# First layer's projections and attention in one block, by half slabs, with five slab slots

## The reference

```python
mod = jnp.dot(jax.nn.silu(c), w_ada[l]) + b_ada[l]          # 6 x 1024 modulation values
h = rmsnorm(x, g_pre_mix[l]) * (1.0 + sc1) + sh1
z = jnp.dot(h, w_in[l])                                      # q_m k_m v_m o_m i_m f_m q_a kc vc ks vs kw vw g_a
qk = jax.nn.silu(causal_depthwise_conv(concat(q_m, k_m), conv_qk[l]))
y_m = mlstm(q_m, k_m, v_m, i_m + b, f_m + b) * jax.nn.sigmoid(o_m)          # 4 heads of 128
kc, vc = compress(kc_a, ...), compress(vc_a, ...)            # 15 compressed keys and values
y_a = nsa(q_a, kc, vc, ks, vs, kw, vw, sigmoid(g_a), rel_bias)              # 8 heads of 64, three branches
y = jnp.dot(concat(y_m, y_a), w_out[l])
x = x + gt1 * rmsnorm(y, g_post_mix[l])
h2 = rmsnorm(x, g_pre_ffn[l]) * (1.0 + sc2) + sh2
x = x + gt2 * rmsnorm(moe(h2, ...), g_post_ffn[l])           # 32 experts, top 4
# second_block: its own modulation from ada_w_2, projections, sparse attention, state-space branch
```

## Time and profile before

| what | us |
|---|---|
| runs of the kernel before, median (lowest to highest) | 1987.55 (1986.05 to 1988.58) |
| the profiled execution, its own time | 1990.91 |
| its span | 1988.9 |
| PE busy / DVE / ACT / POOL | 1822.5 / 456.5 / 319.3 / 74.4 |
| mean granted clock of PE, as a share of full speed | 0.95 |

### The profile page before, as it was taken

The page is one execution under the profiler, slowest core; times in us unless marked ns, Lnnn a source line. Parts: engine busy times, 40 slices in busy tenths (PEclk is TensorE's granted clock), DMA queues, the critical chain, the costliest instruction groups (busy, mean ns, idle before and its releaser), DMA issues. The chain is left out here.

```text
span 1988.9 us, 37739 instructions
## 1 busy us (share of the span) xinstructions
PE 1822.5 (92%) x16443; PEld 1012.4 (51%) x16443; DVE 456.5 (23%) x718; ACT 319.3 (16%) x628; POOL 74.4 (4%) x57
## 2 busy tenths in 40 slices
PE   7996576799999999999999999999949898899998
PEld 5685345433434343434344443434425787667886
DVE  1223504511101010111111111111231550443301
ACT  1102412400000000000000000000020265222200
POOL 0000000000000000000000000000000034100000
PEclk9997787799999999999999999999969899899999
DMA  8964741689999999999999999999644233132410
GB/s 283 245 234 133 269 164 36 279 341 393 397 403 391 398 401 397 402 399 399 394 404 395 405 394 404 399 397 413 260 161 165 89 127 127 43 127 103 151 43 22
DMA packets 159951, 546.34 MB, mean 275 GB/s; under 512 B 24682, under 2 KB 35194, under 8 KB 127002
## 3 DMA queue, kind: packets, MB, share of 16 engines
q1 hardware_dynamic: 136960, 524.32, 68.8%
q10 hardware_dynamic: 21786, 17.09, 2.9%
q0 software_dynamic: 1152, 4.19, 0.6%
HBM read 527.09 MB, written 17.84 MB: 274 GB/s over the span
## 5 line engine op out<-in xcount | busy, mean ns | idle before, releaser
L1319 PE MATMUL ps<-ring_low,xg 128*32 128x512 f32 x3072 | 346.8, 600 | 0.0
L1319 PE MATMUL ps<-second_ring,xg 128*32 128x512 f32 x3072 | 335.4, 592 | 0.0
L1319 PEld LDWEIGHTS ps<-second_ring,xg 128*32 128x32 f32 x3072 | 99.5, 110 | 230.1 <-issue 230.1
L1319 PEld LDWEIGHTS ps<-ring_low,xg 128*32 128x32 f32 x3072 | 97.0, 111 | 208.7 <-issue 203.0
L1450 DVE TENSOR_SCALAR gl<-ps 128x768 f32<-128x768 f32 x32 | 30.6, 958 | 686.9 <-PE ps L1319 686.9
L1342 PE MATMUL ps<-second_ring,aT 128*32 128x256 f32 x3072 | 173.3, 382 | 2.3 <-ACT aT L1401 2.3
L1342 PE MATMUL ps<-raw_more,aT 128*32 128x256 f32 x3072 | 171.6, 379 | 0.0
L1342 PEld LDWEIGHTS ps<-second_ring,aT 128*32 128x32 f32 x3072 | 100.4, 111 | 82.5 <-issue 20.2
L1342 PEld LDWEIGHTS ps<-raw_more,aT 128*32 128x32 f32 x3072 | 99.9, 110 | 65.9
L1395 ACT ACTIVATE sg<-gl 128x768 f32<-128x768 f32 x32 | 27.0, 845 | 512.2 <-DVE gl L1450 512.2
L277 PE MATMUL ps<-hT,second_ring 128*128 128x256 f32 x448 | 98.2, 380 | 1.5 <-PEq L1549 1.5
(11 more groups left out here) (469 smaller groups left out, 1665.0 us busy)
## 6 DMA issues: line engine op xcount, KB each, us to landing
ring_low<-in_w_up_dram SPq DMA_DIRECT2D x128, 1024.0 KB, 6.8
second_ring<-in_w_up_dram SPq DMA_DIRECT2D x128, 1024.0 KB, 6.7
second_ring<-in_w_down_dram SPq DMA_DIRECT2D x64, 1024.0 KB, 6.8
raw_more<-in_w_down_dram SPq DMA_DIRECT2D x64, 1024.0 KB, 7.4
second_ring<-in_w_in_dram SPq DMA_DIRECT2D x11, 2048.0 KB, 8.0
ring_low<-in_w_in_dram SPq DMA_DIRECT2D x10, 2048.0 KB, 8.4
first_ring<-in_w_ada_dram SPq DMA_DIRECT2D x7, 2048.0 KB, 8.8
ring_low<-in_w_ada_dram SPq DMA_DIRECT2D x5, 2048.0 KB, 16.4
```

Source lines behind the costliest of these rows:

```text
L1319: mm = pe.matmul(ps[32 * q:32 * q + 32, u, :], xg[:, k, 32 * block_of:32 * block_of + 32], w[:, :, 256 * f:256 * f + 256], start=False, st ...
```

## The change

- The projection block and the attention block become one block. Five slots in place of six; the order of use is a new list `USE1`, in which modulation slabs stand between projection slabs, and the projections come as qa, kv, tok, q, k, v, o. The eight modulation slabs of `w_ada` stay in the joined block, the six of `ada_w_2` move into the output block, behind and between the slabs of `w_out`.
- PE makes each projection slab in two halves of one bank each (`half(i)`, banks 0 and 1 in turn), with pieces of the attention between the halves. From the third half on, a half waits until ACT has taken the half two before (`in_taken`).
- The halves are copied out of `ps` by ACT (`take(i)`), no longer by DVE. o is taken with the sigmoid. ACT's eleven small DMAs are still first in its list, ahead of `take(0)`. The swaps of `kc4` are now issued by ACT too.
- The modulation rows are sent by POOL, no longer by SP. In the output block POOL also issues the fill of `y_dram`, ahead of these rows.
- `LM1`, `L0`, `WT0` and `zc` get places apart from the tiles with which they were shared; the convolution is written straight into `qkT`.
- At the end of the expert block SP issues two slabs of the second layer in place of four, then waits for the last gathers (`got0`), then issues the other three.

```diff
-SLOTS, SLOTS2 = 6, 5
+SLOTS, SLOTS2 = 5, 5
...
+USE1 = [("mod", m) for m in range(4)]
+USE1 += [("in", "qa"), ("in", "kv"), ("in", "tok"), ("mod", 4), ("mod", 5), ("in", "q"), ("mod", 6), ("mod", 7), ("in", "k"),
+         ("mod", 8), ("mod", 9), ("in", "v"), ("mod", 10), ("mod", 11), ("in", "o")]
+USE1 += [("out", 0), ("mod", 12), ("out", 1), ("mod", 13), ("mod", 14), ("mod", 15), ("mod", 16), ("mod", 17)]
...
+FIRST_SLABS = 5
...
         with nc.Block() as block:
+            @block.sync
+            def _(sp):
+                for n in range(FIRST_SLABS, N_OF["in", "o"] + 1 + SLOTS):
+                    load_slab(sp, n, SLABS1[n])
+            @block.gpsimd
+            def _(pool):
+                for m in range(4, 12):
+                    mod_row_send(pool, m, 4)
+            @block.scalar
+            def _(act):
+                act.dma_start(bgate[:], bass.AP(A["b_gates"].tensor, 0, [[0, P], [1, 8]])).then_inc(sm("small_in"), 16)
+                for par in range(2):
...
+                        act.dma_start(wck[at, :, 64 * twice:64 * twice + 64],
+                                      A["w_cmp_k"][every].rearrange("l d e -> d l e")).then_inc(sm("small_in"), 16)
+                    act.dma_start(wcv[at, :, :], A["w_cmp_v"][every].rearrange("l d e -> d l e"))\
+                        .then_inc(sm("small_in"), 16)
...
+                            act.dma_start(posT[at, kind, :], A[name][every].rearrange("l d -> d l"))\
+                                .then_inc(sm("small_in"), 16)
+                def take(i):
+                    name, h = HALVES1[i]
+                    if h:
+                        act.wait_ge(sm("slab_used"), N_OF["in", name] + 1)
+                    else:
+                        act.wait_ge(sm("in_half"), i // 2 + 1)
...
+                    S.done(act, act.activation(dst, src, ACT.Sigmoid if name == "o" else ACT.Copy), sm("in_taken"))
...
+                take(0)
+                take(1)
+                take(2)
+                swap(kvx, 0, "kvx_in")
+                table_copy(0)
+                take(3)
+                swap(ksw, 2, "ksw_in")
+                table_copy(1)
+                take(4)
+                take(5)
...
+            @block.tensor
+            def _(pe):
+                def half(i):
+                    name, h = HALVES1[i]
+                    n = N_OF["in", name]
+                    if h == 0:
+                        pe.wait_ge(sm(f"slab_ready{n % len(slots)}"), slab_count(SLABS1, n))
+                    if i >= 2:
+                        pe.wait_ge(sm("in_taken"), i - 1)
...
+                half(0)
+                half(1)
+                half(2)
+                flip(0)
+                half(3)
+                flip(1)
+                half(4)
+                half(5)
+                mod(4)
+                scores(0)
...
             with nc.Block() as block:
+                @block.gpsimd
+                def _(pool):
+                    pool.dma_start(y_dram[0:TOTAL, :].rearrange("(p a) d -> p a d", p=P),
+                                   cst[:, 0:D].unsqueeze(1).to_broadcast([P, TOTAL // P, D])).then_inc(sm("rows_filled"), 16)
+                    for m in range(12, 18):
+                        mod_row_send(pool, m, 12)
+                    pool.wait_ge(sm("rows_filled"), 16)
...
+                    for i in range(2):
+                        n = N_OF["out", i]
+                        pe.wait_ge(sm(f"slab_ready{n % len(slots)}"), slab_count(SLABS1, n))
+                        columns_by_tokens(pe, n, 2 * i, src=mix).then_inc(sm("slab_used"), 1)
+                        mod(12 + i)
+                    mod(14)
+                    norm_sums(pe, sq, 4, "x_summed", 2)
+                    mod(15)
+                    mod(16)
+                    mod(17)
+                    norm_sums(pe, sq, 5, "x_summed", 3)
...
                 sp.wait_ge(s("", "up_used"), NE * UPS)
-                for n in range(4):
+                for n in range(2):
                     load_slab(sp, n, SLABS2[n], "b_")
                 sp.wait_ge(s("", "down_used"), NE * DOWNS)
-                load_slab(sp, 4, SLABS2[4], "b_")
+                for t in range(TT):
+                    sp.wait_ge(s("", f"got0{t}"), 16)
+                for n in range(2, SLOTS2):
+                    load_slab(sp, n, SLABS2[n], "b_")
```

More of the change, by code:

```diff
@@ L100, in shape_constants @@
     c[:, C_PICK] = np.arange(P) % 32 == 0
-    for r in range(7 * 16):
+    for r in range(P):
         c[r, C_SUM4 + 4 * (r // 16) + r % 4] = 1
@@ L354, in _ @@
                     sp.dma_start(xtok[:], A["x"].rearrange("(t p) d -> p t d", p=P)).then_inc(sm("x_in"), 16)
-                    for n in range(5):
+                    for n in range(FIRST_SLABS):
                         load_slab(sp, n, SLABS1[n])
@@ new lines, in _ @@
+                dve.wait_ge(sm("in_taken"), 6)
+                V.link(dve, dve.tensor_tensor(gt[:], tokz[:, :, 0:8], bgate[:].unsqueeze(1).to_broadcast([P, TT, 8]),
+                                              ALU.add))
+                V.done(dve, dve.scalar_tensor_tensor(nab[:], f, -1.0, f, ALU.mult, ALU.min), sm("nab_ready"))
+                logits(0)
+                dve.wait_ge(sm("ln_ready"), 1)
+                V.done(dve, dve.scalar_tensor_tensor(lf[:], f, 0.0, nab[:], ALU.min, ALU.subtract), sm("lf_ready"))
@@ new lines, in _ @@
+                dve.wait_ge(sm("compressed"), 1)
+                for g in range(2):
+                    V.link(dve, dve.tensor_copy(kcm[:, g, :], ps[:, 7, g * NCMP:(g + 1) * NCMP]))
+                    ins = dve.tensor_copy(vcm[:, g, :], ps[0:NCMP, 7, AD * (g + 1):AD * (g + 2)])
+                    (V.done(dve, ins, sm("kcm_ready")) if g else V.link(dve, ins))
+                probs(0)
+                conv(0, 0)
+                logits(1)
+                dve.wait_ge(sm("f_summed"), 1)
+                V.link(dve, dve.tensor_copy(F[:].rearrange("p t h -> p (t h)"), ps[:, 7, 256:256 + 2 * MH]))
@@ new lines, in _ @@
+                for par in range(2):
+                    sc = ps[:, 5 + par, 0:TT * 4 * NCMP].rearrange("p (t n) -> p t n", t=TT)
+                    out_l = Lc[:, :, 4 * par:4 * par + 4, :].rearrange("p t s i -> p t (s i)")
+                    in_b = cbias[:, :, 4 * par:4 * par + 4, :].rearrange("p t s i -> p t (s i)")
+                    ins = dve.scalar_tensor_tensor(out_l, sc, AD ** -0.5, in_b, ALU.mult, ALU.add)
+                    (V.done(dve, ins, sm("c_copied")) if par else V.link(dve, ins))
@@ L953, in two_layers @@
+                V.link(dve, dve.tensor_tensor(mod[:, 16:48], ps[:, 7, 0:32], colv("b_ada")[:, 16:48], ALU.add))
         att.close()
```

896 lines of the change are left out of this document (431 added, 465 removed).

## The result

The changed kernel took 1941.83 us, the median of four runs (1940.59 to 1946.39), beside 1986.8 for the kernel before on the same chip: ratio 0.978, 95% interval 0.976 to 0.980. The forecast was 1950 in a range of 1932 to 1972. The profiled execution had a span of 1940.3 us and an own time of 1942.06. That is 48.6 us of span less than before, where the sum had said 37.6.

A forecast was written before the change was run, and what follows sets the result against it. PE bounds projections and experts; in the attention nothing is full and engines wait in turn. Joined block -38.2, output block +6.3, experts' end -5.7 sum to -37.6: 1987.55 us becomes 1950, range 1932 to 1972.

The forecast's parts named there:

- The likeliest case: Whole kernel: the forecast's own sum, median 1950 us, own bounds 1934 to 1964, chance 0.62.
- (1) first slab: Start of the joined block: slab qa takes 15.7 us from 53.1, done at 68.8.
- (2) the hold: Joined block behind qa: PE waits for ACT's first take, behind ACT's DMA issues; stands still 26.9 us, goes on at 95.7.
- (3) from there to the output block: Rest of the joined block: slabs and modulation rows, remaining attention, waits and end; output block starts at 246.7.
- (4) output block: Output block: extra modulation row, later second norm and POOL's sends add 6.3 us; router starts at 308.8.
- (6) experts' end: End of the expert block: last store and gathers run without SP's later slabs beside them, -5.7 us, bounds -3 and -9.
- the slow stretch: Within ACT's hold: the remaining 2460 pieces pass beside wide slab pieces, 16.5 us from 79 to 95.5.
- The two waits that the walk found: PE in the joined block: 3.7 us for `a_ready` behind mod(5), 2.1 us of mod(9) for ACT's copy of row 8.
- ACT not being held: Joined block rival: the issues run off while ACT takes, PE has no 26.9 us stop; 1923 us, chance 0.06.
- Lists that wait more: Joined block rival: ACT's and DVE's in-order lists wait 10 to 25 us more than walked; 1967 us, chance 0.17.
- POOL's queue late: Output block rival: POOL's fill and sends take double, +10 to +15 us; 1963 us, chance 0.09.
- The low clock: Joined block rival: short stops keep PE at its lower clock level; 2043 us with slabs and rows low, chance 0.04.

The follow-up runs named there:

- e10: The kernel before, with two of ACT's ten small DMAs fewer and the doubled columns of wck copied by DVE: 1987.8 us, ratio 1.0001 to the kernel before.
- e6: The changed kernel with the small DMAs, two fewer, issued by POOL only once slabs kv and tok have landed: 1918.0 us.
- e5: The changed kernel with two of ACT's ten small DMAs fewer, the doubled columns of wck copied by DVE: 1928.16 us.
- e4: The changed kernel with slab tok loaded as one wide part in place of four narrow ones (values not the reference's): 1946.74 us.
- e1: The changed kernel with ACT's eleven small DMAs issued by POOL in the same order: 1928.27 us.
- e2: The changed kernel with the experts' end as before, SP issuing second-layer slabs without waiting for the last gathers: 1948.64 us.
- e8: The changed kernel with four slots in the first layer's ring in place of five: 1939.6 us.
- e7: e5 with the last two of the eight remaining small DMAs issued behind ACT's first two takes: 1920.01 us.
- e9: e6 with PE's two remaining waits filled by parts of projection halves: 1912.87 us.

## Why the prediction was right, and where it was not

The likeliest case came true, and 1941.83 lies 8.2 us below its 1950, inside that case's own bounds (1934 to 1964). Step by step, in us of span:

| step | predicted | measured |
|---|---|---|
| (1) first slab | done at 68.8 | 70.1 |
| (2) the hold: PE goes on at | 95.7 | 90.9 |
| (3) from there to the output block | 151.0 | 151.0 |
| joined block in place of two | -38.2 | -43.0 |
| (4) output block | +6.3 | +3.4 |
| (5) experts | 0 | -1.9 |
| (6) experts' end | -5.7 | -4.3 |
| second layer | 0 | -2.8 |
| sum | -37.6 | -48.6 |

**The hold** was the right mechanism with one term of the wrong size. The 43.74 us that ACT had spent on issues in the kernel before stopped nobody there (PE was busy 95.81 of 96 us, and e10's shorter hold won nothing) and turned into a stop of PE here. It goes when ACT no longer issues them (e6), shrinks with fewer pieces (e5), grows with wider neighbours (e4). The mis-sized term is the count of pieces left for the slow stretch. The prediction had ACT's queue at 5720 by 79; it had passed 6247 by 76, at 370 a us over 60 to 76 where 300 had been taken. Also, it needed some 8070 pieces gone where 8200 had been taken. So the slow stretch began 3 us sooner and had 1820 pieces in it, not 2460. It took 14 us, not 16.5, and would have taken 12 at the rate of 149 a us: between 76 and 80 the queue went slower than that (324 pieces). Only for e4 and e5 was the better rule used (one piece for each of SP's), and it gave both stops to within 3.5 us.

The Trainium skill ("DMA: Bandwidth & Descriptors", section on issuing engines not being separate DMA queues) calls the sequencer time of starting a DMA usually small beside the transfer. For POOL's issues this trace agrees (0.84 us each in e1). For ACT's issues of 1024 pieces it does not: 37 us for eleven of them.

**From the restart to the output block** the walk gave 151.0 us (its own terms add up to 150.8) and the trace shows 150.95. So close a match is luck: with the same code from there on the stretch took 150.0 to 152.1 in e1, e2, e4 and e8, and not each term was exact. The two waits that the walk found are where it put them, at 3.9 and 3.2 us (3.7 and 2.1 predicted), and nothing else makes PE wait. The compressions took 7.5 us, not 6.3. The half behind the stop lost 2.9, not 1.8. The 1.7 us that each short wait was to cost the work behind it came true here (1.4 and 1.7), but not as a rule: behind the second wait it was nothing in e2, e5, e7 and e8. The other groups made up for it. e6 and e9 show that the waits are real: filling both made the block 6.4 us shorter. That the joined block wins its time by projection work that stands in the old waits, and by the clock that follows, is read from the two traces (PE idle 46 us before, 29.5 now with the stop); no run took the joining apart.

**Slots and slabs** cost nothing, as said; e8 shows it for the joined block with one slot less still.

**The output block** was put 2.9 too high. Modulation row 12 cost its 1.9. The first slab took 14.05 us and not 15.7, though with the same code it took 15.74 in five experiments and 17.07 in e9: that size moves from run to run. The second norm's sums ended 7.2 us behind the second slab, 3.9 before: +3.3 where 1.4 was given, as PE does rows 13 and 14 (3.64 us) first. The +3 for POOL's queue was nothing: its sends took 0.52 us each where SP's took 0.61, and `mod2` was written 0.5 us before ACT's last shift ended. From the second norm's `rstd` to the router it was 22.0 us, 22.2 before. Together -1.7 + 1.9 + 3.3 - 0.2 = +3.3 us, the measured 3.4 but for rounding, with errors of 2 to 3 us in both directions inside one small term: the size is near by luck in part.

**Experts and second layer** are unchanged code. -1.9 and -2.8 are what such stretches differ by between executions: from the router to the last store 1095.4 to 1100.6 us in the kernels shown, from the second layer's first matmul to the end 504.5 to 508.3. Within the second layer a few groups of PE's matmuls differ by their mean alone (the q-k scores took 408 ns each before and 375 after). The profiled execution of before lay 3.4 over the median of its runs and that of after did not, so the medians moved by 45.0 and not 48.6. Set against the forecast's 37.6, about 5 us are the hold and 3 the output block; the rest cancels.

**The experts' end** was right in mechanism and a little large in size (-5.7, and 5.8 by its own terms; -4.3 here, -1.6 to -4.5 in the other kernels with the changed order and end). The first gather followed the last store after 5.2 us, where 4 had been taken from the swaps; the rest of the way was as said.

**One reading** was wrong and harmless: the issue of 3.38 us that the prediction puts between 84 and 88 ran from 93.10; the one that ran from 85.56 took 3.50.

**The rivals.** ACT not being held is refuted, by the 20.8 us for which PE waited for ACT's first take and by e5 and e6. Lists that wait more: 7.1 us of waits, no more. POOL's queue late: not here. The low clock: the opposite happened. The rows took 1.92 us, but for one of 2.63 behind its wait, and the clock was 0.92 to 1.00 in the windows from the restart on (0.72 in the first 10 us, 91 to 101); the 10.6 us come from it.

Left open: whether POOL's queue would matter with a longer backlog, since the margin was 0.5 us and no run doubled it; why ACT's queue went so slowly between 76 and 80; and why the opening block took 2.5 to 4 us less in the experiments, in either kernel.

## What to carry to other kernels

Idle time of an engine that reads "issue" is not free time: when a change gives that engine something that others wait for, its DMA issues become their wait. Before such a change, count the pieces of its DMAs, issue fewer (e5), issue them behind the first thing that others need (e7), or give them to an idle engine and hold them back until the transfers that are wanted first have landed (e6). And test a moved queue by its neighbours: giving ACT's DMAs to POOL at once took the hold away, and POOL's packets made a wait for kv instead (e1).

## What the runs showed of the hardware

- Two queues with work (ACT's and SP's) passed their pieces one for one over long stretches, whatever their sizes: 594 to 592 beside 2 KB pieces, 1343 to 1337 beside narrow ones, 6247 to 6316 over 23 us. Single stretches of 4 us went up to a fifth or a quarter either way, and one to 324 against 591. So a small piece pays the time of its neighbour's large one. The Trainium skill ("DMA: Bandwidth & Descriptors", section on queues, rings and completion order) says that each engine goes round-robin between queues at packet granularity; the even counts agree, with one piece of ACT's counted as one packet by the profile.
- An issue held ACT once about 2100 pieces of its queue were under way (10,240 less the 8070 that had gone when ACT came free; 1790 to 2500 at the ends of the held issues before). Up to there it took 0.9 us for 1024 pieces, beyond it as long as the queue needed for them, 2.5 to 7.2. Ten such DMAs from POOL held it for 0.84 us each (e1).
- POOL's plain DMAs of the same 256-byte pieces went in packets of 2.2 KB at 0.29 us each (e1), 0.13 us of an engine for a KB, where ACT's queue took 0.177 x 64 / 594 = 0.019 us for a piece of 256 bytes, 0.076 for a KB.
- PE's stops of 6.5 to 29.0 us made the half behind them 1.5 to 2.9 us longer (8.55 to 9.97 in place of 7.07), and not by their length: 9.85 behind 6.5 us (e1), 8.55 behind 29.0 (e4). A stop of 1.7 us (e7) cost next to nothing, 7.14. The wait of 3.9 us cost the spreads behind it 1.3 to 1.7 more (3.33 to 3.78 in place of the 2.05 of e9, which waited 0.3). The wait of 3.1 cost the row and the half behind it 1.3 to 1.7 in four kernels and nothing in e2, e5, e7 and e8.
